# A mixture-of-experts loop: six single units to a unit of four, a ring of 30 places, two gather buffers, the final weights loaded late

## What is computed

```python
s = sigmoid(x @ w_router); sel = s + b_router
# the best 4 of 8 groups, then the top 8 of 64 experts; weights normalised, times 2.5
hg = einsum('nd,edf->nef', x, w_gate); hu = einsum('nd,edf->nef', x, w_up)
hid = silu(hg) * hu * combine[:, :, None]          # D_EXPERT = 256
y = einsum('nef,efd->nd', hid, w_down)
sh = (silu(x @ w_sh_gate) * (x @ w_sh_up)) @ w_sh_down
h = h + g2 * (y + sh); out = rmsnorm(h, final_norm_g)
```

## Time and profile before

| | us |
|---|---|
| three runs | 1134.74, 1127.90, 1129.11 (median 1129.11) |
| the profiled execution | 1130.05 |
| its span | 1128.2 |
| mean granted clock of TensorE | 0.969 of full |
| up to the expert loop's first weighting | 602.8 |
| the last weighting (L1773) starts | 1084.5 |

### The profile page before, as it was taken

The page is one execution under the profiler, slowest core; times in us unless marked ns, Lnnn a source line. Parts: engine busy times, 40 slices in busy tenths (PEclk is TensorE's granted clock), DMA queues, the critical chain, the costliest instruction groups (busy, mean ns, idle before and its releaser), DMA issues.

```text
span 1128.2 us, 15199 instructions
## 1 busy us (share of the span) xinstructions
PE 1033.6 (92%) x4895; PEld 711.8 (63%) x4895; DVE 546.0 (48%) x1110; ACT 364.8 (32%) x484; POOL 158.3 (14%) x134
## 2 busy tenths in 40 slices
PE   5999999999999999999989999799799699798875
PEld 2599888788888987945545545356355355355442
DVE  1423443456789848735535434244244143254358
ACT  3334543337444365102323223122122131132201
POOL 0022221000000000000012214023123013033200
PEclk9999999999999999999999999799899899899988
DMA  9999864357344343621569999999999999967592
GB/s 387 418 265 352 100 95 85 150 210 258 151 150 150 151 150 95 239 74 38 230 248 387 373 420 414 411 416 378 424 403 381 418 397 375 396 277 260 224 390 114
DMA packets 68593, 306.12 MB, mean 271 GB/s; under 512 B 13924, under 2 KB 18148, under 8 KB 54720
## 3 DMA queue, kind: packets, MB, share of 16 engines
q1 hardware_dynamic: 49248, 270.57, 60.5%
q0 software_dynamic: 11968, 26.35, 10.3%
q10 hardware_dynamic: 7328, 8.55, 2.2%
HBM read 284.72 MB, written 36.32 MB: 285 GB/s over the span
## 4 chain that ended last, share of the span: by engine, by line
PE 43%; DMA 11%; SPq 5%; issue 2%; DVE 2%; ACT 2%; POOLq 0%; DVEq 0%; ACTq 0%; POOL 0%
PE PS L2202 14%; DMA bigA<-in_w_down 6%; PE PS L2088 4%; PE PS L1836 3%; SPq L727 3%; PE PS L2223 2%; PE PS L2188 2%; PE PS L2225 2%; PE PS L2224 2%; DMA bigB<-in_w_down 2%; DMA bigB<-in_w_gu 2%; PE PS L2159 2%; PE PS L2298 2%; SPq L722 1%; DMA nT<-n_rows,IDX 1%
## 5 line engine op out<-in xcount | busy, mean ns | idle before, releaser
L2202 PE MATMUL PS<-bigB 128*128 128x512 f32 x272 | 127.7, 609 | 2.7 <-DMA bigB<-in_w_gu 2.7
L1232 POOL DMA_INDIRECT y_parts<-bigB,IDX x37 | 77.1, 2085 | 361.0 <-DVE bigB L1773 349.2
L2202 PE MATMUL PS<-bigA,bigB 128*128 128x512 f32 x232 | 105.7, 597 | 0.0
L1890 PE MATMUL PS<-bigB_r 128*128 128x384 f32 x288 | 99.0, 344 | 1.3 <-ACT bigB L917 1.3
L1892 PE MATMUL PS<-bigB_r,bigA_r 128*128 128x384 f32 x288 | 96.8, 336 | 0.0
L1891 PE MATMUL PS<-nT_r,bigB_r 128*128 128x384 f32 x288 | 96.7, 336 | 0.0
L1773 DVE TENSOR_SCALAR bigB<-PS,bigD 128x1024 f32<-128x1024 f32 x39 | 50.0, 1283 | 92.7 <-PE PS L2225 79.0
L2223 PE MATMUL PS<-bigC_r,bigB_r 128*128 128x512 f32 x132 | 66.1, 501 | 25.3 <-DVE bigB_r L1754 25.3
L1381 DVE TENSOR_TENSOR bigA_r<-bigA,bigB_r 128x2048 fp32r<-128x2048 f32 x18 | 41.6, 2309 | 97.3 <-ACT bigB_r L943 97.3
L2202 PEld LDWEIGHTS PS<-bigB 128*128 128x128 f32 x272 | 50.3, 195 | 53.3 <-issue 50.4
L917 ACT ACTIVATE bigB<-PS 128x384 f32<-128x384 f32 (+1 forms) x55 | 27.3, 497 | 142.5 <-PE PS L1892 71.1
(11 more groups left out here) (381 smaller groups left out, 2073.2 us busy)
## 6 DMA issues: line engine op xcount, KB each, us to landing
bigA<-in_w_in SPq DMA_DIRECT2D x17, 2048.0 KB, 12.1
bigB<-in_w_gu SPq DMA_DIRECT2D x14, 2048.0 KB, 22.1
bigB<-in_w_gu SPq DMA_DIRECT2D x50, 512.0 KB, 12.3
bigA<-in_w_down SPq DMA_DIRECT2D x20, 1024.0 KB, 22.5
bigA<-in_w_ada SPq DMA_DIRECT2D x8, 2048.0 KB, 9.0
bigA<-in_w_down SPq DMA_DIRECT2D x30, 512.0 KB, 12.8
bigA<-in_w_gu SPq DMA_DIRECT2D x7, 2048.0 KB, 20.9
bigA<-in_w_gu SPq DMA_DIRECT2D x27, 512.0 KB, 14.6
```

The lines of the kernel that those rows point to most:

```text
L1232: pool.indirect_dma_start(y_parts, bass.IndirectOffsetOnAxis(ap=IDX[:, p, 1:2], axis=0), YS[:, p % 2, :], None, bounds_check=T * TOPK - 1, ...
L1890: mm(out, wh, nh, start=(k == 0), stop=False)
L2202: last = mm(PS[:, 2 + b, :], XT[:, b, k, :], PIECE[RING_AT["gu", c][k // 2]][:, half], start=first, stop=stop)
```

## The change

`PERIOD, BIGS` become 7, 6; a quad comes after six bigs. `RING` becomes 30; three places are added (a second one in `bigD`, one in `bigB` where final_g lay, and the first 1024 columns of `nT`, which was the third gather buffer). The new order of a period is gu0, qdn, gu1, dn0, gu2, dn1, gu3, dn2, gu4, dn3, gu5, dn4, qgu, dn5: 60 places, two turns; SyncE's waits are rewritten to fit. `XGS` and `GAHEAD` go from 3 to 2. final_g is loaded after the last unit's gate_up, and its reader in the final norm waits for it. The reads of `y_parts` are in another order of buffers, nine instead of seven of them ahead of the wait for the last down. The core of the diff:

```diff
-PERIOD, BIGS = 6, 5
+PERIOD, BIGS = 7, 6
-RING = 27
+RING = 30
-XGS, AHEAD, GAHEAD = 3, 4, 3
+XGS, AHEAD, GAHEAD = 2, 4, 2
...
-        XG = [bigB[:, 19968:20992], bigB[:, 20992:22016], nT_flat[:, 0:D]]
+        XG = [bigB[:, 19968:20992], bigB[:, 20992:22016]]
...
-                   + [(bigB, bigB_r, 4096 + i * D) for i in range(2)] + [(bigD, bigD_r, 0)]
-                   + [(bigB, bigB_r, 17920 + i * D) for i in range(2)])
+                   + [(bigB, bigB_r, 4096 + i * D) for i in range(2)] + [(bigD, bigD_r, i * D) for i in range(2)]
+                   + [(bigB, bigB_r, 12800), (nT_flat, nT_r, 0)] + [(bigB, bigB_r, 17920 + i * D) for i in range(2)])
...
-              + [cut(bigA, i, (2, D)) for i in (0, 2048, 6144, 8192)] + [cut(nT_flat, D, (2, D))])
-        YG_FREE = 7
+              + [cut(bigA, i, (2, D)) for i in (6144, 8192, 0, 2048)] + [cut(nT_flat, D, (2, D))])
+        YG_FREE = 9
...
-                        sp.dma_start(FG, final_g.partition_broadcast(P)).then_inc(fin_loaded, 16)
...
             sp.wait_ge(te_ready, 1)
             f = number(3)
             big_gate_up(f, 3, GU_TO[3][0:2])
+            big_down(e, 2)
+            sp.wait_ge(sg_ready, NT)
+            big_gate_up(f, 3, GU_TO[3][2:])
+            e = number(4)
+            sp.wait_ge(shd_ready, NT)
+            big_down(f, 3)
+            f = number(5)
+            big_gate_up(f, 5, GU_TO[5])
             sp.wait_ge(gu_ready, 1)
-            big_gate_up(f, 3, GU_TO[3][2:])
-            big_down(e, 2)
-            sp.wait_ge(shd_ready, NT)
-            e = number(4)
             big_gate_up(e, 4, GU_TO[4])
-            big_down(f, 3)
+            sp.wait_ge(sh_added, NT)
+            big_down(e, 4)
             with sp.If(1 <= quads):
                 experts = quad_numbers(RTAB - 4)
-                sp.wait_ge(sh_added, NT)
-                quad_slices(experts, 0, range(3))
                 sp.wait_ge(gu_ready, 2)
-                quad_slices(experts, 0, range(3, 4))
-                sp.wait_ge(dn_ready, 1)
+                quad_slices(experts, 0)
+                sp.wait_ge(gu_ready, 3)
                 quad_slices(experts, 1)
-                sp.wait_ge(gu_ready, 3)
+                sp.wait_ge(dn_ready, 2)
                 quad_slices(experts, 2)
                 sp.wait_ge(gu_ready, 4)
                 quad_slices(experts, 3)
-            sp.wait_ge(gu_ready, 4)
-            big_down(e, 4)
+            sp.wait_ge(dn_ready, 3)
+            big_down(f, 5)
...
             sp.wait_ge(gu_ready, units)
+            sp.dma_start(FG, final_g.partition_broadcast(P)).then_inc(fin_loaded, 16)
...
             gather(0, 0)
             gather(1, 1)
-            pool.wait_ge(sg_ready, NT)
-            link(nc.gpsimd.memset(XG[2], 0.0))
-            gather(2, 2)
             pool.wait_ge(xg_t, 1)
             gather(GAHEAD, GAHEAD)
...
-                    dve.wait_ge(fin_loaded, 48)
+                    dve.wait_ge(fin_loaded, 32)
...
                 rsqrt_fix(col(4), col(8), col(12), col(24))
+                dve.wait_ge(fin_loaded, 48)
```

## The result

The changed kernel takes 1173.57 us in the median (1172.07 to 1175.78, 4 runs), the kernel before 1129.8 beside it (1127.9 to 1134.74): a ratio of 1.038, with an interval of 1.034 to 1.042. It is slower, and 18.6 us above the 1155 forecast. The profiled execution of after has a span of 1170.2 us against 1128.2; these 42.0 us are divided here.

The account below looks back on a forecast made before the run. DMA was taken to bound four periods of the loop before, late gathers after: 602.5 + 75 + 388 + 16 = 1081.5, plus 30.8 to the last weighting at 1112.3, 27.8 later; span 1156, less one, 1155 us; range 1122 to 1174.

Parts of the forecast that it names:

- The bound of before: Expert loop: four periods of 81 us bound by DMA, 12 to 13 us of waiting in each.
- Gathers with two buffers: Expert loop: gathers issued 5.7 us into a step, room down from 16.5 to 5.4 us, so TensorE's transposes stall.
- the sum: Loop, transposes of unit 3 (602.5) to those of unit 37 (1081.5): 75 + 388 + 16 us.
- the 10.7 us taken: Loop: assumed time of one gather in the 14 later pairs of steps, 27.7 us a pair.
- The clock: Loop: TensorE at 1.2 GHz after stalls, 1.7 us at two of three late pairs, 16 us; bounds 0 and 24.
- the forecast's 416 us: Loop, first to last weighting: TensorE's work after the change if nothing were late, against 481.7 us before.
- The first rival: Loop: bytes decide, gathers fall to about 5 us; last weighting 1050 to 1063, about 1101 us; chance 0.15.
- the fourth rival: Loop: gathers stay near 13.4 us, every stall at slow clock, 32.1 us a pair, 1190 us; chance 0.05.
- the first pairs: Loop's beginning: 3 pairs of steps with gathers of 7.9 us while DMA catches up, 3 x 24.9 = 75 us.
- The start: Before the loop: earlier weights gain nothing until DMA binds; gather 2 is at most 1 us late.
- At nothing: Parts expected to cost nothing: final_g (1.3 us if not hidden), y_parts reads, one wait fewer, early gather (at most 1 us).
- gathers in full: Loop: the main forecast, late gathers stall TensorE, 1155 us, its own range 1142 to 1172; chance 0.6.

Follow-up runs that it names:

- The second profile of after: The changed kernel profiled once more with nothing altered, to see how far executions differ: 1177.47 us, loop 520.5 us.
- shifted by 72: Changed kernel with 72 never-executed instructions placed ahead of VectorE's loop, its 351-instruction body kept: 1172.97 us, ratio 1.035 to the kernel before.

## Why the prediction was right, and where it was short

**The bound of before, and what the change does to it**: right. Down weights no longer hold the loop, DMA is at 0.89 to 0.93 in it, and periods last 98 to 100 us (forecast some 100).

**Gathers with two buffers**: right in place, and in size by two errors that cancel. Issue 5.7 us into the step, 15 waits (forecast 15 to 20) of up to 7.6 us. From the transposes of unit 3 to those of unit 37 the sum had 75 + 388 + 16 = 479 us; after takes 481.2 (606.3 to 1087.5). That these agree so well is in part luck, for the split within the sum was off both ways and cancelled. Of the 479, 384 are work (34 steps of 11.3) and 79 stalls; measured are 60.6 us of waiting for rows. Gathers were a bit shorter than the 10.7 us taken: thirty of them from 659.9 on average 10.0. The clock cost more than the 16 us:

```profile
606.30:1087.46 481.16, 415.50 (x1735) 230.84 (x1733) 167.44 (x326) 116.33 (x132) 119.48 (x68) 0.93 0.90 353
```

TensorE is busy for 415.5 us there, 31 over the 384 of work, and 5.0 us more go to two waits for an index product: 384 + 31 + 60.6 + 5.0 is the 481. The two rows of the whole loop, after's and then before's, give both clocks:

```profile
606.60:1119.00 512.40, 442.10 (x1821) 247.25 (x1819) 182.41 (x355) 122.94 (x140) 125.11 (x70) 0.92 0.88 343
```

```profile
602.80:1084.50 481.70, 432.42 (x1834) 241.88 (x1832) 183.19 (x361) 121.90 (x143) 111.64 (x71) 0.95 0.94 374
```

Over the forecast's 416 us for the loop TensorE is busy 26 us more in after and 16 us more in before (with one empty place in it); and the 416 aren't pure work, since before's last two steps, from which they are worked out, hold the wait of 4.49 us, so that the true excess is some 31 and 21. The forecast added its clock to steps at full speed, and its upper bound of 24 was too low. The granted clock fell from 0.95 to 0.92, by the kind of stall forecast. From the transposes of unit 37 to the last weighting 31.5 us pass (30.8 forecast).

**The first rival** (bytes decide) isn't what happened, but the runs show its sum was good: with the gathers out of the way and the jumps fast the last weighting is at 1064.1, where it had 1050 to 1063. The sum of the fourth rival was not: by its own terms 75 us for the first pairs and 14 pairs of 32.1 give a time of some 1200, not 1190.

**The start**, where nothing was to be gained and at most 1 us lost, came out as +3.8 us in the profile of after. TensorE is at 1.2 GHz twice ahead of the loop, without having waited any longer than before:

```profile
545.00:580.00 35.00, 31.46 (x101) 16.37 (x100) 11.36 (x31) 6.35 (x13) 2.44 (x2) 0.90 0.85 348
580.00:606.00 26.00, 24.00 (x83) 14.05 (x82) 8.18 (x18) 7.05 (x8) 2.27 (x2) 0.93 0.79 298
```

In before both stretches have a clock of 1.00 with the same busy time. The second profile of after has none of it, and its first weighting is at 603.4. Over the kernels with the change it lies at 603.1 to 606.7, over those without at 602.3 to 602.8. So some 0.6 to 0.8 us are the change's own, as forecast, and the other 3 come and go between executions. What starts them is open; of the eight profiles with the change four have one at 552, of the five without it none.

**"At nothing", the end**: this is a step that failed, though the time stayed inside the range. It asked what final_g, the reads of y_parts and one wait could cost, and found cover for each; it didn't ask what two more steps in each pass do to the program's length, nor what the extra skipped pass costs. The tail was 7.6 us longer: the one-hots start 11.6 us after the last weighting instead of 5.75 (6.0 for the slow jump, 0.8 for the fifth skipped pass, 0.9 back because fewer steps are skipped one by one), and the product behind TensorE's wait of 9.0 us takes 8.82 us, 1.8 more than at 2.4 GHz. With the jump fast the tail is 44.7 to 44.9 against 43.7; that product's clock is still in it (8.75 us behind a wait of 2.9, shifted by 72), and no wait for the final weights or the reads shows, as said.

Together, for the span: 1156 forecast, 3.8 for the start, 2.2 and 0.7 in the loop, 7.6 at the end, 1170.3; measured 1170.2. That profiled execution took 1172.39 us in all, 1.2 below the median of its kernel. The median of 1173.57 is only 0.4 us inside the range's upper end of 1174, and above the 1142 to 1172 that the forecast gave for gathers in full: the cause was right, but 11.4 us of start and tail, which stood at nothing to 1 us, lie on top of it.

## What to carry to other kernels

Before a buffer is given up, work out from the in-order queue that fills it at which point of a step its transfer is issued and how many steps remain; the number of buffers and the number of steps ahead are two settings, and here only the second cost anything (31 us alone, 52 us in the changed kernel). A transfer that is short when DMA idles must be costed at what it takes when DMA is full. When a loop's body grows, look at each engine's jump back in the profile, with the count of instruction packets: here a few instructions too many held VectorE for some 6 us per pass, of which the kernels paid between nothing that shows and all, and moving the loop by 72 made its jumps short again.

## What the hardware showed that was not expected

- VectorE's jump back took 0.3 us or 5.3 to 6.4 us, nothing in between, by the length of its loop and its place in the program; three or four blocks of 128 instructions is a rule that fits. 50 instructions of code that mostly isn't run made the kernel 19 us slower.
- Ahead of the loop TensorE's granted clock fell to 1.2 GHz in some executions and not in others (one stretch of 6.8 us from 551.7, one of 3.4 us from 585.8, in the profile of after), behind the same small matmuls and the same waits of 0.6 to 1.1 us, and cost 3 us at the first weighting.
- In the loop that waits for gathers, taking two pauses of 5.6 us away from VectorE gave nothing back that shows (523.3 against 512.4 and 520.5 us); in the loop that doesn't, it gave 11 us in the time, with the one behind the loop.
